# Retention, forgetting and stick-breaking attention in float32: the totals of the last 16 keys in one half-height matmul for each bank, the forgetting tail in column groups

## The chip, the cores and the metric

The kernel runs on one NeuronCore of one Trainium2 chip. The metric is the device time of one execution in microseconds (us). Before the change it is 1461.64 us, the median of 3 runs (1461.39 to 1462.56).

## The reference

The input is 256 tokens of 1024 features. The first block puts 16 learned tokens ahead of them (272 in all), and then comes a mixer of two halves, retention with 4 heads and forgetting attention with 8 heads, and a gated feed-forward network with a short convolution. The second block puts 16 other learned tokens in place of the first and runs two layers, each with a feed-forward network, a mixer (stick-breaking attention with 8 heads of 64, beside a convolution over 31 tokens) and another feed-forward network. All of it is float32. Two parts matter here:

```python
# stick-breaking attention, second block, 8 heads, 2 layers
z = jnp.einsum('bhqd,bhkd->bhqk', qb, kh) * scale
valid = key_pos < qpos
log_keep = jnp.where(valid, jax.nn.log_sigmoid(-z), 0.0)
after = lax.cumsum(log_keep, axis=3, reverse=True) - log_keep
attn = jnp.where(valid, jnp.exp(jax.nn.log_sigmoid(z) + after), 0.0)

# forgetting attention, first block, 8 heads
logits = jnp.einsum('bqhd,bkhd->bhqk', qf[:, q0:q1], kf[:, :q1]) * scale
bias = c[:, :, q0:q1, None] - c[:, :, None, :q1]
logits = jnp.where(mask[None, None], logits + bias, NEG)
p = jax.nn.softmax(logits, axis=-1)
outs.append(jnp.einsum('bhqk,bkhd->bqhd', p, vf[:, :q1]))
```

## The kernel before, in words

**The projections.** Each weight slab (1024 x 128, or 1408 x 128) is split into a rounded high part (`whi`, type fp32r, by ScalarE) and a rounded low part (`wlo`, by VectorE or GpSimd), and so are the activations (`xh`, `xl`). A product is then three single-pass fp32r matmuls for every 128 rows: L1685, L1686 and L1687. These make up most of the program. Each engine has its own instruction stream, written out by hand in Python; semaphores join the streams. There is no scheduler: the order in the streams is the order in the code.

**Where the small matmuls stand.** All other work of TensorE is put between the slabs at fixed slab numbers `s`. 272 tokens are three blocks of 128, 128 and 16. Attention for the last block, of 16 keys or 16 queries, is the tail. Small matmuls go through a helper `mm` (L1837), so the trace shows that line for nearly all of them; the tiles and shapes tell them apart. The scratch tensor `scr` holds, among others, `prob`, `probT`, `qz`, `keep` and `attn`; `ax` holds the split activations and, at that time, `keep_hi` and `keep_lo`. XP and XQ are two PSUM tiles of two banks each, called X[0] to X[3].

**Stick-breaking attention** (`mixer`, four slabs or phases for each pair of heads c, from slab 14 on; in the prediction such a turn is a round). `scores(c)` writes the logits of two heads into X[0] and X[1]: keys on the partitions, 432 columns for the three key blocks. ScalarE and VectorE turn them into `keep` (minus the log of the keep factor). ScalarE rounds it to `keep_hi` (L870) and GpSimd makes `keep_lo`, the rest (L518). `sums(c)` adds the reverse cumulative sum over keys: four matmuls of 432 columns with a triangle of -1 (`later_r`), then the totals of later key blocks with a matrix of -1 (`minus_r`): four of 144 columns and four of 32 columns. The last four bring the total of the last 16 keys to the 16 last queries of the two earlier blocks. Their right-hand side is 128 rows high, though only 16 rows hold keys; the others hold zeros. `values(c)` multiplies with the values. In these phases VectorE also evacuates each slab, and runs the 31 taps of the convolution (L1488) in the time that is left.

**Forgetting attention, the tail.** The 16 last queries of all 8 heads are put side by side on 128 partitions (`qz`, zero outside each head's own 16 columns). `tail_logits` (slab 14) adds a mask, the decay and four matmuls of 272 columns, one for each pair of heads, all into the 128 x 272 output. `tail_values(c)` (slabs 18 to 21) multiplies the 128 value features of a pair of heads with the 32 probability columns of that pair, three matmuls for the three key blocks; the part that mixes one head's features with the other's queries is never read.

A matmul may take fewer than 128 rows of weights (lower height, a row group) or fewer than 128 columns (a column group, whose output goes to the same partitions). The kernel already does so in `scores` (two heads, 64 rows each), in the retention's `ret_products` (four heads, 32 rows each), and in `fox_values` and `values` (two heads, 64 columns each).

Of the kernel before, what the change touches and what calls it, by code (L numbers as in the profile page):

```python
# [27 lines left out]
F32 = mybir.dt.float32  # L28
F32R = mybir.dt.float32r
ALU = mybir.AluOpType  # L30
ACT = mybir.ActivationFunctionType


P = 128
# [3 lines left out]
T = META + SEQ  # L38
# [7 lines left out]
CC = 4  # L46
# [15 lines left out]
SBW, SB_SEG = 432, 144  # L62

FOX_A, FOX_B, FOX_W = slice(0, P), slice(P, 3 * P), 3 * P
# [112 lines left out]
FV, FQ, FK, RQ, RK, RV, RG = 0, 4, 5, 12, 14, 16, 20  # L177
# [5 lines left out]
def build(nc, hT, meta2, w8, w11, fbias, prm_d, cst1_d, cst_d, gain_d, out_d):  # L183
    ctx = ExitStack()
    with ctx:
        def sb(name, shape, dt=F32):
            return ctx.enter_context(nc.sbuf_tensor(name, shape, dt))
# [24 lines left out]
        eps = sb("eps", [P, 3])  # L212
        tok_sum, tok_pre, tok_rec = sb("tok_sum", [P, 5]), sb("tok_pre", [P, 3]), sb("tok_rec", [P, 2])
        acc = sb("acc", [P, T])
        sq = sb("sq", [P, 2, T])
        rinv = sb("rinv", [P, T])
        gmix = sb("gmix", [P, 2 * DC])
# [240 lines left out]
        @block.gpsimd  # L458
        def _(pool):
            def lo(g, j, cols):  # L460
                pool.wait_ge(hi_ready[j], g + 1)
                pool.tensor_tensor(wlo[:, j, 0:cols], raw[:, j, 0:cols], whi[:, j, 0:cols].bitcast(F32),  # L462
                                   ALU.subtract).then_inc(lo_ready[j], 1)

            def los(n, g, kind):
                cols, slots = kind
                with pool.Fori(0, n) as i:
                    for j in slots:
                        lo(g + i, j, cols)

            def first_los(g):

                for j in SHARED:
                    lo(g, j, S8)

            for k, value in enumerate((EPS, EPS * EPS, LN_EPS)):
                pool.memset(eps[:, k:k + 1], value).then_inc(eps_set, 1)
            wff = prm[:, PRM_WFF:PRM_WFF + DC * FOX_H]
            pool.wait_ge(prm_landed, 16)
            pool.tensor_copy(wffr[:, 0, :], wff).then_inc(gate_step, 1)  # L480
            pool.wait_ge(gate_step, 1)
            pool.tensor_tensor(wffr[:, 1, :], wff, wffr[:, 0, :].bitcast(F32), ALU.subtract).then_inc(gate_step, 1)
            lo(0, 2, S8)
            lo(0, 3, S8)
            lo(1, 0, S8)
            lo(1, 1, S8)
            pool.wait_ge(ff_step, 2)
            lo(1, 2, S8)
            pool.wait_ge(cst_landed, 16)
            pool.tensor_copy(identr[:, :], ident).then_inc(hide_ready, 1)  # L490
            pool.tensor_copy(hider[:, :], hide).then_inc(hide_ready, 1)
            pool.tensor_copy(later_r[:, :], minus_later).then_inc(hide_ready, 1)
            pool.tensor_copy(selr[:, :], ident[0:P, 0:FOX_H]).then_inc(gate_step, 1)
            pool.wait_ge(gate_step, 3)
            pool.tensor_copy(selr[FOX_LO, :], ident[FOX_LO, FOX_LO]).then_inc(gate_step, 1)
            pool.wait_ge(gate_step, 4)
            pool.tensor_copy(tailr[:, :].rearrange("p (h q) -> p h q", h=FOX_H),
                             selr[:, :].bitcast(F32).rearrange("p (h q) -> p h q", q=1).to_broadcast(
                                 [P, FOX_H, T - 2 * P])).then_inc(mask_ready, 1)
            pool.memset(qz[:, :, :], 0.0).then_inc(qz_zero, 1)  # L500
            pool.memset(proj[:, FQ:FK + 2 * CC - 1, 0:T_A], 0.0).then_inc(q_zero, 1)
            lo(1, 3, S8)
            pool.wait_ge(c1_landed, 16)
            pool.tensor_copy(fmaskr, fmask).then_inc(mask_ready, 1)
            pool.tensor_copy(minus_r[:, :], minus_ones).then_inc(minus_ready, 1)
            los(N_QKV1 - 2, 2, K8A)
            los(1, G_WO1, K8A)
            los(N_DN, G_DN1, K11)
            first_los(G_LAYER)
            for l in range(LAYERS):  # L510
                g = G_LAYER + PER_LAYER * l
                los(N_UP - 1, g + L_UPA + 1, K8S)
                los(N_DN, g + L_DNA, K11)
                with pool.Fori(0, CC) as c:
                    for j in range(3):
                        lo(g + L_MIX + LOW_FROM + c, j, S8)
                    pool.wait_ge(keep_high, CC * l + c + 1)
                    pool.tensor_tensor(keep_lo, keep, keep_hi.bitcast(F32), ALU.subtract).then_inc(keep_low, 1)  # L518
                    lo(g + L_MIX + LOW_FROM + c, 3, S8)
                los(N_UP - 1, g + L_UPB + 1, K8S)  # L520
                if l < LAYERS - 1:
                    los(N_DN, g + L_DNB, K11)
                    first_los(g + PER_LAYER)
                    continue
                for n in range(LAST_SLABS):
                    if n % 4 in SHARED:
                        lo(g + L_DNB + n // 4, n % 4, S8)
# [3 lines left out]
        def _(act):  # L531
# [312 lines left out]
            def mixer(g, l, p, t):  # L844
# [21 lines left out]
                def round_keep(c):  # L866
                    act.wait_ge(keep_ready, CC * l + c + 1)
                    if c:
                        act.wait_ge(cum_mm, CC * l + c)
                    act.activation(keep_hi, keep, ACT.Copy).then_inc(keep_high, 1)  # L870

                def weights(c):

# [131 lines left out]
        def _(dve):  # L1005
# [463 lines left out]
            def mixer(g, l, p, t):  # L1469
# [21 lines left out]
                def keeps(c):  # L1491

                    dve.wait_ge(soft_step, 3 * (CC * l + c) + 3)
                    dve.scalar_tensor_tensor(keep, XP[:, :, 0:SBW], 0.0, keep, ALU.max, ALU.add).then_inc(keep_ready, 1)

                def out_lo(c):
                    dve.wait_ge(o_hi, CC * l + c + 1)
                    dve.tensor_tensor(al[:, c, t:], X[2][:, t:T], ah[:, c, t:].bitcast(F32), ALU.subtract).then_inc(o_lo, 1)

                ga = g + N_MIX  # L1500
                for s in range(4 * N_MIX):
# [47 lines left out]
                                          ALU.mult).then_inc(u_ready, 1)  # L1549
                    if phase == 1 and 0 <= pair < CC:  # L1550
                        keeps(pair)
                    if s < LN_FROM:
                        taps(s)

# [117 lines left out]
        def _(pe):  # L1672
# [163 lines left out]
            def mm(out, lhsT, rhs, start):  # L1836
                return pe.matmul(out, lhsT, rhs, start=start, stop=True, skip_group_check=True)  # L1837
# [94 lines left out]
            def tail_logits():  # L1932
                pe.wait_ge(fp_ready, 2 * FOX_PAIRS)
                pe.wait_ge(qz_ready, 2 * CC)
                pe.wait_ge(c_ready, 6)
                out = X[0][:, 0:T]
                mm(out, identr[:, :], fmaskr[:, FOX_W:], True)
                mm(out, tailr[:, :], csumr, False)
                for c in range(CC):
                    ins = mm(out, qz[:, c, :], proj[:, FK + 2 * c, :], False)  # L1940
                ins.then_inc(fl_mm, 1)

            def fox_turn(i):
# [27 lines left out]
            def tail_values(c):  # L1971

                pe.wait_ge(rs_ready, 6 if c else 2)
                if c >= 2:
                    pe.wait_ge(ro_sq, c - 1)
                w = 2 * (T - 2 * P)
                for b in range(3):
                    ins = mm(X[3][:, FOX_W + w * c:FOX_W + w * c + w], vT[:, b, P * c:P * c + P],
                             probT[:, 0, P * b + w * c:P * b + w * c + w], b == 0)
                if c == CC - 1:  # L1980
                    ins.then_inc(fo_mm, 1)

# [116 lines left out]
            def mixer(g, l, t):  # L2099
# [18 lines left out]

                def sums(c):

                    pe.wait_ge(keep_low, CC * l + c + 1)
                    tail, mid = T - 2 * P, SB_AT[0] + P
                    for part in (keep_hi, keep_lo):
                        for bank in range(2):
                            mm(X[bank][:, 0:SBW], later_r[:, :], part[:, bank, :], False)
                    if c == 0:
                        pe.wait_ge(minus_ready, 1)
                    for part in (keep_hi, keep_lo):
                        for bank in range(2):
                            mm(X[bank][:, mid:SB_AT[1]], minus_r[:, :], part[:, bank, SB_AT[1]:SBW], False)  # L2130
                    for part in (keep_hi, keep_lo):
                        for bank in range(2):
                            both = X[bank][:, mid:SBW].rearrange("p (s n) -> p s n", n=SB_SEG)[:, :, P:SB_SEG]
                            last = part[:, bank, 0:tail].rearrange("p (s n) -> p s n", s=1).to_broadcast([P, 2, tail])
                            ins = mm(both, minus_r[:, :], last, False)
                    ins.then_inc(cum_mm, 1)

                def values(c):
# [204 lines left out]
```

## Time and profile before

| | |
|---|---|
| median of 3 runs | 1461.64 us |
| profiled execution | 1462.14 us |
| its span | 1460.3 us |
| VectorE busy | 903.3 us (62%) |
| ScalarE busy | 767.8 us (53%) |
| GpSimd busy | 493.8 us (34%) |
| TensorE clock granted | 0.999 of full |
| DMA | 250.92 MB, mean 172 GB/s |

In the profile PE is TensorE (matmuls), PEld its weight loads, DVE VectorE, ACT ScalarE, POOL GpSimd. Busy time is the union of an engine's instructions over the span. The end of a matmul in the profile is modelled, and matmuls overlap, so the time that one costs is read from the start or the end of one to that of the next. Of the profiled execution's 1462.14 us the span covers 1460.3 us.

### The profile page before, as it was taken

To read this page: it belongs to the slowest core of one execution; us is meant where nothing else is said; L and a number is where in the kernel's file an instruction comes from. 1 tells how busy PE (TensorE), PEld (TensorE's weight loads), DVE (VectorE), ACT (ScalarE), POOL (GpSimd) and SP (SyncE) were. 2 spreads that over 40 slices of the span, in tenths; PEclk is the share of its full clock that TensorE was granted. 3 is DMA by queue.
4 is the path that set the end of the run, shared out by engine and by line. 5 is a ranking of instruction groups with operands and counts; after the bars stand their busy time and mean duration, and the time that the engine had idled before them with its cause. 6 is when DMAs were issued, how large, how long until landed. Compare 5 with 4: busy or idle time off the path is not lost.

```text
span 1460.3 us, 30910 instructions
## 1 busy us (share of the span) xinstructions
PE 1452.9 (99%) x11465; PEld 1421.6 (97%) x11465; DVE 903.3 (62%) x1576; ACT 767.8 (53%) x1097; POOL 493.8 (34%) x212
## 2 busy tenths in 40 slices
PE   9999999999999999999999999999999999999998
PEld 8999999889999999999999999999999999999987
DVE  6438888756445469988644434444447898864533
ACT  6556565555444446567544544444444657654443
POOL 6551000533334303710333442433420570044342
PEclk9999999999999999999999999999999999999999
DMA  7435566645556445445555654555644545567663
GB/s 262 137 102 160 176 196 192 213 157 172 173 172 212 163 130 165 141 156 162 175 176 172 207 180 129 183 173 183 199 151 145 173 118 186 174 193 202 208 189 114
DMA packets 74635, 250.92 MB, mean 172 GB/s; under 512 B 15809, under 2 KB 16705, under 8 KB 74561
## 3 DMA queue, kind: packets, MB, share of 16 engines
q1 hardware_dynamic: 74272, 249.38, 54.6%
q8 instruction: 49, 0.80, 0.2%
q10 hardware_dynamic: 288, 0.54, 0.1%
q14 instruction: 26, 0.20, 0.0%
HBM read 247.79 MB, written 1.05 MB: 170 GB/s over the span
## 4 chain that ended last, share of the span: by engine, by line
PE 98%; DVE 1%; ACT 0%; issue 0%; DVEq 0%; ACTq 0%
PE W L1685 27%; PE W L1686 27%; PE W L1687 27%; PE W L1773 3%; PE XP L1837 3%; PE XQ L1837 2%; PE W L1772 1%; PE W L1737 1%; PE W L1788 1%; PE W L1787 1%; PE W L1738 1%; PE W L1786 1%; PE W L1739 1%; PE XQ L1949 0%; PE XP L1842 0%
## 5 line engine op out<-in xcount | busy, mean ns | idle before, releaser
L462 POOL TENSOR_TENSOR wlo<-raw,whi 128x1024 fp32r<-128x1024 f32 (+1 forms) x185 | 473.2, 2562 | 915.4 <-ACT whi L536 914.9
L1685 PE MATMUL W<-xh,whi 128*128 128x272 f32 (+2 forms) x2400 | 689.8, 287 | 0.0
L1686 PE MATMUL W<-xl,whi 128*128 128x272 f32 (+2 forms) x2400 | 687.0, 286 | 0.0
L1687 PE MATMUL W<-xh,wlo 128*128 128x272 f32 (+2 forms) x2400 | 685.9, 286 | 0.0
L536 ACT ACTIVATE whi<-raw 128x1024 fp32r<-128x1024 f32 (+1 forms) x440 | 480.9, 1098 | 128.9 <-PE W L1687 89.6
L1685 PEld LDWEIGHTS W<-xh,whi 128*128 128x128 f32 x2400 | 452.3, 188 | 2.2 <-issue 1.2
L1687 PEld LDWEIGHTS W<-xh,wlo 128*128 128x128 f32 x2400 | 452.1, 188 | 0.0
L1686 PEld LDWEIGHTS W<-xl,whi 128*128 128x128 f32 x2400 | 451.3, 188 | 0.2
L1011 DVE TENSOR_TENSOR wlo<-raw,whi 128x1024 fp32r<-128x1024 f32 (+1 forms) x255 | 331.7, 1302 | 80.5 <-ACT whi L536 80.1
L1685 PE MATMUL W<-ax,whi 128*128 128x272 f32 (+2 forms) x816 | 234.4, 287 | 0.4 <-DVE ax L1455 0.3
L1686 PE MATMUL W<-ax,whi 128*128 128x272 f32 (+2 forms) x816 | 234.4, 287 | 0.0
L1687 PE MATMUL W<-ax,wlo 128*128 128x272 f32 (+2 forms) x816 | 234.3, 287 | 0.0
L1686 PEld LDWEIGHTS W<-ax,whi 128*128 128x128 f32 x816 | 154.8, 190 | 0.0
L1685 PEld LDWEIGHTS W<-ax,whi 128*128 128x128 f32 x816 | 153.6, 188 | 0.9 <-issue 0.5
L1687 PEld LDWEIGHTS W<-ax,wlo 128*128 128x128 f32 x816 | 153.4, 188 | 0.0
L1027 DVE TENSOR_TENSOR scr<-W,rinv 128x272 f32<-128x272 f32 (+2 forms) x140 | 60.3, 431 | 113.7 <-PE W L1687 113.1
L586 ACT ACTIVATE ax<-W 128x272 f32 (+3 forms) x88 | 34.7, 395 | 180.4 <-DVE W L1098 180.4
L583 ACT ACTIVATE scr<-scr 128x272 f32<-128x272 f32 (+1 forms) x110 | 46.9, 426 | 107.8 <-DVE scr L1027 76.5
L1027 DVE TENSOR_TENSOR W<-W,rinv 128x272 f32<-128x272 f32 (+1 forms) x88 | 39.1, 444 | 93.3 <-PE W L1687 93.3
L1488 DVE SCALAR_TENSOR_TENSOR XQ<-scr,prm,XQ 128x272 f32<-128x272 f32 (+1 forms) x184 | 91.3, 496 | 5.3
L560 ACT ACTIVATE sq<-h 128x272 f32 (+3 forms) x48 | 20.4, 426 | 99.9 <-DVE h L1046 99.9
L1046 DVE SCALAR_TENSOR_TENSOR h<-W,h 128x272 f32<-128x272 f32 (+3 forms) x48 | 20.7, 434 | 80.0 <-PE W L1687 78.0
(288 smaller groups left out, 1405.1 us busy)
## 6 DMA issues: line engine op xcount, KB each, us to landing
raw<-in_w SPq DMA_DIRECT2D x377, 512.0 KB, 3.7
raw<-in_w SPq DMA_DIRECT2D x64, 704.0 KB, 4.1
proj<-proj SPq DMA_DIRECT2D x16, 64.0 KB, 3.6
scr<-in_cst SPq DMA_DIRECT2D x1, 1000.0 KB, 8.6
h<-in_hT SPq DMA_DIRECT2D x3, 272.0 KB, 5.2
raw<-in_w SPq DMA_DIRECT2D x2, 256.0 KB, 4.1
proj<-in_gain SPq DMA_DIRECT2D x1, 512.0 KB, 4.6
out<-proj SPq DMA_DIRECT2D x4, 128.0 KB, 1.8
```

Of the source, the lines that this page charges most:

```text
L462: pool.tensor_tensor(wlo[:, j, 0:cols], raw[:, j, 0:cols], whi[:, j, 0:cols].bitcast(F32), ALU.subtract).then_inc(lo_ready[j], 1)
L536: act.activation(whi[:, j, 0:cols], raw[:, j, 0:cols], ACT.Copy).then_inc(hi_ready[j], 1)
L583: act.activation(actv[:, b, t:], gate[:, b, 2 + t:T + 2], ACT.Silu).then_inc(act_ready, 1)
L586: act.activation(ah[:, bass.ds(c, 1), t:], gated(b, conv, t), ACT.Copy).then_inc(ah_ready, 1)
L1011: dve.tensor_tensor(wlo[:, slot, 0:cols], raw[:, slot, 0:cols], whi[:, slot, 0:cols].bitcast(F32), ALU.subtract).then_inc(lo_ready[slot], 1)
L1027: return dve.tensor_tensor(out, W[bank][:, t:T], rinv[:, t:], ALU.mult)
L1488: ins = dve.scalar_tensor_tensor(total, u[:, c, k + t:k + T], w, total, ALU.mult, ALU.add)
L1685: pe.matmul(out, whi[:, j, w], mh, start=start and k == 0, stop=False, skip_group_check=True)
L1686: pe.matmul(out, whi[:, j, w], ml, start=False, stop=False, skip_group_check=True)
L1687: ins = pe.matmul(out, wlo[:, j, w], mh, start=False, stop=stop and k == len(rhs) - 1, skip_group_check=True)
L1773: ins = pe.matmul(both, whi[:, j, w], ax[:, c, :, T_B:], start=False, stop=c == FC - 1, skip_group_check=True)
L1837: return pe.matmul(out, lhsT, rhs, start=start, stop=True, skip_group_check=True)
```

## The change

There are three parts.

1. A new tile `keep_last`, 128 x 16, holds for bank 0 in its rows 0 to 63 and for bank 1 in its rows 64 to 127 the first 32 rows of the last key block's `keep`: 32 rows rounded (ScalarE, two instructions behind `keep_hi`) and 32 rows of the rest (VectorE, two subtractions in `last_lo`, behind the evacuation of phase 2). The four matmuls of `sums` with 128 rows become two with 64 rows, one for each bank. `keep_high` and `keep_low` count three steps for each pair in place of one, and the sums wait for both.
2. `tail_logits`: the matmul of head pair c takes only the 32 columns of `qz` that belong to it and writes only its 32 partitions.
3. `tail_values`: each matmul becomes two, one for each head, of 64 weight columns and 16 columns of probabilities.

```diff
         acc = sb("acc", [P, T])
+        keep_last = sb("keep_last", [P, T - 2 * P], F32R)
...
-                    pool.wait_ge(keep_high, CC * l + c + 1)
+                    pool.wait_ge(keep_high, 3 * (CC * l + c) + 1)
...
                     act.activation(keep_hi, keep, ACT.Copy).then_inc(keep_high, 1)
+                    for bank in range(2):
+                        act.activation(keep_last[64 * bank:64 * bank + 32, :], keep[0:32, bank, 0:T - 2 * P],
+                                       ACT.Copy).then_inc(keep_high, 1)
...
+                def last_lo(c):
+
+                    dve.wait_ge(keep_high, 3 * (CC * l + c) + 1)
+                    if c:
+                        dve.wait_ge(cum_mm, CC * l + c)
+                    for bank in range(2):
+                        dve.tensor_tensor(keep_last[64 * bank + 32:64 * bank + 64, :], keep[0:32, bank, 0:T - 2 * P],
+                                          keep_hi[0:32, bank, 0:T - 2 * P].bitcast(F32), ALU.subtract).then_inc(keep_low, 1)
...
+                    if phase == 2 and 0 <= pair < CC:
+                        last_lo(pair)
                     if s < LN_FROM:
                         taps(s)
...
                 for c in range(CC):
-                    ins = mm(out, qz[:, c, :], proj[:, FK + 2 * c, :], False)
+                    rows = slice(32 * c, 32 * c + 32)
+                    ins = mm(out[rows, :], qz[:, c, rows], proj[:, FK + 2 * c, :], False)
...
                 for b in range(3):
-                    ins = mm(X[3][:, FOX_W + w * c:FOX_W + w * c + w], vT[:, b, P * c:P * c + P],
-                             probT[:, 0, P * b + w * c:P * b + w * c + w], b == 0)
+                    for half in range(2):
+                        p0, q0, q1 = 64 * half, w * c + w // 2 * half, w * c + w // 2 * (half + 1)
+                        ins = mm(X[3][p0:p0 + 64, FOX_W + q0:FOX_W + q1], vT[:, b, P * c + p0:P * c + p0 + 64],
+                                 probT[:, 0, P * b + q0:P * b + q1], b == 0)
...
-                    pe.wait_ge(keep_low, CC * l + c + 1)
+                    pe.wait_ge(keep_high, 3 * (CC * l + c + 1))
+                    pe.wait_ge(keep_low, 3 * (CC * l + c + 1))
...
-                    for part in (keep_hi, keep_lo):
-                        for bank in range(2):
-                            both = X[bank][:, mid:SBW].rearrange("p (s n) -> p s n", n=SB_SEG)[:, :, P:SB_SEG]
-                            last = part[:, bank, 0:tail].rearrange("p (s n) -> p s n", s=1).to_broadcast([P, 2, tail])
-                            ins = mm(both, minus_r[:, :], last, False)
+                    for bank in range(2):
+                        p0 = 64 * bank
+                        both = X[bank][:, mid:SBW].rearrange("p (s n) -> p s n", n=SB_SEG)[:, :, P:SB_SEG]
+                        last = keep_last[p0:p0 + 64, :].rearrange("p (s n) -> p s n", s=1).to_broadcast([64, 2, tail])
+                        ins = mm(both, minus_r[p0:p0 + 64, :], last, False)
```

TensorE's stream at the first sums of the first layer, before and then with the change; `keep_low` and `keep_high` are the semaphores of the rounded parts, and the L1685 row is the next slab.

```order
2194 L1837 MATMUL XP<-ax,later_r 128x432 [waits keep_low]
2195 L1837 MATMUL XP<-ax,later_r 128x432 x3
2196 L1837 MATMUL XP<-ax,minus_r 128x144 [waits minus_ready]
2197 L1837 MATMUL XP<-ax,minus_r 128x144 x3
2198 L1837 MATMUL XP<-ax,minus_r 128x2x16 x4
2199 L1685 MATMUL W<-xh,whi 128x272 [waits lo_ready2,evac_done]
```

In the changed program the same place reads:

```order
2194 L1852 MATMUL XP<-ax,later_r 128x432 [waits keep_low,keep_high]
2195 L1852 MATMUL XP<-ax,later_r 128x432 x3
2196 L1852 MATMUL XP<-ax,minus_r 128x144 [waits minus_ready]
2197 L1852 MATMUL XP<-ax,minus_r 128x144 x3
2198 L1852 MATMUL XP<-keep_last,minus_r 128x2x16 x2
2199 L1700 MATMUL W<-xh,whi 128x272 [waits lo_ready2,evac_done]
```

Two of the four small matmuls are gone, the other two read `keep_last`, and the first one of the sums waits for a second semaphore. The line numbers of the changed program are 15 higher here.

VectorE's stream in the same round before the change: the softplus (`soft_step`), the taps (`conv_step`), the evacuation of phase 2 (`proj<-W,rinv`), taps, and the next evacuation.

```order
416 L1494 SCALAR_TENSOR_TENSOR scr<-XP,scr 128x864 [waits soft_step]
417 L1488 SCALAR_TENSOR_TENSOR XQ<-scr,prm,XQ 128x272 [waits conv_step] x5
418 L1536 SCALAR_TENSOR_TENSOR proj<-W,rinv 128x272 [waits mm_done]
419 L1488 SCALAR_TENSOR_TENSOR XQ<-scr,prm,XQ 128x272 [waits conv_step] x4
420 L1027 TENSOR_TENSOR scr<-W,rinv 128x272 [waits mm_done]
```

With the change VectorE's stream there is:

```order
416 L1498 SCALAR_TENSOR_TENSOR scr<-XP,scr 128x864 [waits soft_step]
417 L1492 SCALAR_TENSOR_TENSOR XQ<-scr,prm,XQ 128x272 [waits conv_step] x5
418 L1549 SCALAR_TENSOR_TENSOR proj<-W,rinv 128x272 [waits mm_done]
419 L1506 TENSOR_TENSOR keep_last<-scr,ax 32x16 [waits keep_high]
420 L1506 TENSOR_TENSOR keep_last<-scr,ax 32x16
421 L1492 SCALAR_TENSOR_TENSOR XQ<-scr,prm,XQ 128x272 [waits conv_step] x4
422 L1031 TENSOR_TENSOR scr<-W,rinv 128x272 [waits mm_done]
```

The two subtractions stand between the evacuation and the taps, and the first waits for the rounded part of ScalarE.

## Rows read from the trace of the kernel before

**Rows 1.** The page, parts 1 and 4: busy us, share, passes; the chain by engine.
```profile
PE 1452.9 (99%) x11465; PEld 1421.6 (97%) x11465; DVE 903.3 (62%) x1576; ACT 767.8 (53%) x1097; POOL 493.8 (34%) x212
PE 98%; DVE 1%; ACT 0%; issue 0%; DVEq 0%; ACTq 0%
```

**Rows 2.** TensorE's timeline, scores of pair 1, narrow windows: start, length, shape, passes.
```profile
585.73 0.29 PE L1837 MATMUL XP<-hider,identr 128*128 128x288 f32 x1
585.95 0.50 PE L1837 MATMUL XP<-proj,scr 64*128 64x272 f32 x2
...
586.28 0.40 PE L1837 MATMUL XP<-proj,scr 64*128 64x272 f32 x2
...
585.95 1.10 PE L1837 MATMUL XP<-proj,scr 64*128 64x272 f32 x12
```

**Rows 3.** TensorE's timeline, values of pair 0 and the slab behind them.
```profile
586.98 0.45 PE L1837 MATMUL XQ<-scr,vT 128*64 128x272 f32 x2
...
587.77 0.21 PE L1837 MATMUL XQ<-scr,vT 128*64 128x16 f32 x1
587.90 0.39 PE L1685 MATMUL W<-xh,whi 128*128 128x272 f32 x1
```

**Rows 4.** TensorE's timeline, first passes of the retention's scores.
```profile
82.74 0.50 PE L1837 MATMUL XP<-proj 32*128 32x272 f32 x2
82.75 0.50 PE L1837 MATMUL XQ<-proj 32*128 32x272 f32 x2
```

**Rows 5.** TensorE's timeline, end of the first sums and the slab behind them.
```profile
581.74 0.50 PE L1837 MATMUL XP<-ax,minus_r 128*128 128x144 f32 x3
...
582.38 0.26 PE L1837 MATMUL XP<-ax,minus_r 128*128 128x32 f32 x1
582.49 0.37 PE L1685 MATMUL W<-xh,whi 128*128 128x272 f32 x1
```

**Rows 6.** TensorE's timeline, before and behind the tail values of pair 2.
```profile
92.03 0.29 PE L1687 MATMUL W<-xh,wlo 128*128 128x272 f32 x1
...
92.75 0.48 PE L1837 MATMUL XQ<-scr 128*128 128x272 f32 x1
```

**Rows 7.** TensorE's timeline, the tail's logits and the first transpose behind them.
```profile
69.63 0.28 PE L1837 MATMUL XP<-ax,tailr 128*128 128x272 f32 x1
69.76 2.00 PE L1837 MATMUL XP<-proj,scr 128*128 128x272 f32 x8
...
71.59 0.27 PE L1949 MATMUL XQ<-cst,scr 128*128 128x128 f32 x1
```

**Rows 8.** Groups by form, TensorE: passes, busy us together, mean ns.
```profile
L1837 PE MATMUL XQ<-scr,vT 128*64 128x16 f32 x32 | 2.0, 194 | 0.0
```

**Rows 9.** Groups by form: small operations of ScalarE and VectorE.
```profile
L727 ACT ACTIVATE scr<-proj 64x16 f32<-64x16 f32 x8 | 1.7, 210 | 0.1
...
L1146 DVE TENSOR_TENSOR scr<-scr 128x32 f32<-128x32 f32 x1 | 0.2, 194 | 0.0
...
L1336 DVE TENSOR_TENSOR scr<-scr 128x2 f32<-128x2 f32 x4 | 2.7, 676 | 0.1
```

**Rows 10.** Timelines of four engines, last layer; idle time, releaser in brackets.
```profile
1199.29 1.06 ACT L536 ACTIVATE whi<-raw 128x1024 fp32r<-128x1024 f32 x1 [0.55 <-PE W L1687]
...
1165.57 0.44 DVE L1027 TENSOR_TENSOR scr<-W,rinv 128x272 f32<-128x272 f32 x1 [0.85 <-PE W L1687]
...
1180.97 0.42 DVE L1027 TENSOR_TENSOR proj<-W,rinv 128x256 f32<-128x256 f32 x1
...
1196.39 0.42 DVE L1027 TENSOR_TENSOR proj<-W,rinv 128x256 f32<-128x256 f32 x1 [0.20 <-PE W L1687]
...
1200.19 0.42 DVE L1027 TENSOR_TENSOR proj<-W,rinv 128x256 f32<-128x256 f32 x1
...
1198.82 2.05 POOL L518 TENSOR_TENSOR ax<-scr,ax 128x864 fp32r<-128x864 f32 x1 [3.96 <-ACT ax L870]
...
1201.87 0.94 PE L1837 MATMUL XP<-ax,later_r 128*128 128x432 f32 x4
```

## The prediction

> **What bounds the kernel now.** I read four views, in this order. First the page's busy times and its chain of waits: TensorE is busy 99% of the span and is 98% of the chain that ended last [rows 1]. So a change counts by what it does to TensorE's own stream, and work on the other engines is free unless TensorE comes to wait for it. Second the groups by form, to size the small matmuls. Third the timeline of TensorE in narrow windows, at each of the three places that the diff touches and at the places where the kernel already uses half-height, quarter-height or half-width matmuls: these tell what such a matmul costs and what it costs to go over to it and back. Fourth the timelines of the other three engines just ahead of the sums, for the slack of the new rounding steps.
>
> A plain float32 matmul is two passes in the trace, one with rounded operands (fp32r) is one. A pass is counted here by its end, since passes overlap: 1452.9 us for 11465 passes are 0.127 us from one end to the next [rows 1], although a 272-column pass is 0.29 us long.
>
> **The price of a change of mode.** In the scores, full-height passes are followed by half-height ones. The last full one ends at 585.73 + 0.29 = 586.02; the first two half-height passes, one in each half, start at 585.95 and take 0.50 us where the next two take 0.40, because their weights are loaded first, with nothing beside them [rows 2]. They end at 586.45, so the first pass of the new mode ends its own length plus 0.03 us after the last of the old one. Going back it is the same: the last half-width pass ends at 587.77 + 0.21 = 587.98, the first full one at 587.90 + 0.39 = 588.29, its own 0.29 plus 0.03 [rows 3]. For a 272-column pass that is 0.32 us in place of 0.127: each switch costs 0.2 us. Into half-width passes it is a little less: the half-height passes end at 585.95 + 1.10 = 587.05 and the first two half-width ones at 586.98 + 0.45 = 587.43, own length (0.40) less 0.02 [rows 2, 3]. What the modes give is shown too: passes in different row groups run side by side. The quarter-height passes of four heads, two into XP and two into XQ, start within 0.02 us of each other and all end by 83.25 [rows 4].
>
> The Trainium skill says the same of the switch in TensorEngine Tiling (Array Packing), Key Properties: a change of tiling mode drains the engine; it gives no price. The same page's table of theoretical speedups (up to 2x for a half, 4x for a quarter) knows no such cost, and by it the change would come out as in my second rival. The rows above side with the drain.
>
> **Sums over the last 16 keys** (8 executions: 4 head pairs in 2 layers). Before, four full-height fp32r passes of 32 columns stand behind the last 144-column pass. They start 0.11 us apart (582.38, and the projection's 582.49), not the 0.015 that 32/272 of 0.127 would be, because each waits for 128 columns of weights. From the end of the last 144-column pass (581.74 + 0.50 = 582.24) to the end of the first projection pass (582.49 + 0.37 = 582.86) it is 0.62 us [rows 5]. After, two half-height passes in different row groups take their place: 0.19 us (the length of a small pass, 194 ns for 16 columns [rows 8]) plus 0.01 for the second, plus 0.03 for going over, and then 0.29 + 0.03 for going back: 0.55 us. That is 0.07 us less, and 0.06 in unrounded reading; 8 x 0.06 = 0.5 us less. The trace has no fp32r pass at half height, so the bounds are: with no overlap the second comes 0.11 us later, +0.05 x 8 = +0.4 us; with no price for the switch three intervals of 0.11 go, -0.33 x 8 = -2.7 us. I take -0.5, by the scores, which are the nearest rows.
>
> **Forgetting logits of the tail** (once). Before, eight full passes of 272 float32 columns take 2.00 us, (2.00 - 0.39) / 7 = 0.23 us apart. From the end of the pass before them (69.63 + 0.28 = 69.91) to the end of the first transpose behind them (71.59 + 0.27 = 71.86) it is 1.95 us [rows 7]. After, each head pair writes its own 32 partitions with 32 columns of weights. If all four column groups run side by side, as the four row groups of [rows 4] do, two rounds are left: 0.39 + 0.02 for four starts, less 0.02 for going over (from half-width passes), plus 0.23, plus 0.27 + 0.03 for going back: 0.92 us, 1.0 us less. Bounds: side by side by twos, as the half-width passes show for two groups, 0.46 more, so -0.6; none side by side, 8 x 0.23 as before and two switches, +0.3; no price for the switch, 6 x 0.23 = -1.4. I take -1.0.
>
> How long 32 columns of weights take at full height no row here shows. The Trainium skill, TensorE: Matmul & The Clock Gate, section LDWEIGHTS, has it as columns over 1.2 GHz whatever the rows, so an estimate of 0.03 us, against 0.05 for 64; by it the sum would be 0.03 us better still.
>
> **Values of the tail** (4 executions). Before, six full passes of 32 columns. From the end of the projection before them (92.03 + 0.29 = 92.32) to the end of the first pass behind them (92.75 + 0.48 = 93.23) it is 0.91 us [rows 6]. After, twelve passes of 16 columns with 64 columns of weights, in two column groups: six pairs. The trace has such pairs in the stick-breaking values: 8 groups of four passes take 2.0 us together, 0.25 each, so with 0.19 for a pass and 0.01 for its partner a further pair adds 0.05 [rows 8]. That makes 0.19 + 0.01 - 0.02 + 5 x 0.05 = 0.43, and 0.39 + 0.03 for going back (0.39 is the length of such a pass once its weights lie ready, as in the logits): 0.85 us, 0.06 less. Where the transposes follow instead, in the first of the four, I count nothing. I take -0.1 for all four, rounded down. Bounds: twelve passes in a row at 0.05, 0.27 more each, +0.8; no price for the switch, where six steps of 0.11 become 0.05, -0.3 each, -1.2.
>
> **What lies beside.** ScalarE gets two rounding copies of 32 x 16 behind the big one, 16 in all. The nearest row has 0.21 us for 64 x 16 [rows 9], so 0.42 a round, and ScalarE then idles 0.55 us before its next weight rounding [rows 10]: covered. VectorE gets two subtractions a round, between the evacuation and the taps (order rows in the section on the change); the nearest row has 0.19 us for 128 x 32 [rows 9], 0.38 a round. Queued behind them are taps and later evacuations. VectorE's idle time, in which it caught up, is 0.85 us before the second round's softplus in the last layer, then none that the view shows, and 0.20 [rows 10]. So it falls behind by 0.38, then 0.56, and with the fourth pair 0.94 us. TensorE wants the pieces at 1201.87, VectorE's evacuation in the same round begins at 1200.19 and takes 0.42: 1.26 us of lead [rows 10]. GpSimd's low part ends at 1198.82 + 2.05 = 1200.87, 1.0 us ahead, and would be 0.56 late. TensorE waits for neither. The added semaphore wait stands in front of the same matmul as the old one, and behind it is only TensorE's own stream. If this cover were gone, each us of lateness at the fourth sums would be one us of the total.
>
> **The sum.** -0.5 - 1.0 - 0.1 = -1.6 us. The profiled execution took 1462.14 us (span 1460.3), so 1460.5; the median of before is 0.5 us below that execution, so on the scale of the medians 1461.64 - 1.6 = 1460.0 us. This is 0.1%, inside the 0.2% (2.9 us) that a measurement of this kernel can tell from no change.
>
> **Rivals.** *The pieces do not overlap.* Only plain float32 passes are seen side by side, in two or four row groups or two column groups; fp32r and four column groups are not. Then each split only adds passes and switches: +0.4 + 0.3 + 0.8 = +1.5 us, 1463.1, slower than before. Against it: every tiled pass in the trace overlaps. It decides once the pieces that run one after the other cost more than the 1.6 us of the forecast, so over half of them.
> *The switch costs nothing here.* For it: the weights are the same minus_r that is already loaded in full, and the switch's price is seen only with plain float32 on its tiled side. Then -2.7 - 1.4 - 1.2 = -5.3 us, 1456.3: faster. Against it: the row of the scores has a price although fp32r stands ahead, and the way back leads into fp32r.
> *VectorE is late.* Among its small operations one kind takes 0.68 us for 128 x 2 [rows 9]. At that price a round costs 1.36 us; in the last layer it is behind by 0.51, 1.87, 3.03, and 4.39 with the fourth pair, less 1.26 of lead: TensorE waits 3.1 us by the fourth sums, and at most as much in the layer before, of which I take two thirds. With the 1.6 gained, 3.1 + 2.1 - 1.6 = +3.6 us, 1465.2: slower. It decides from 6x - 0.20 = 1.26, x = 0.24 us for one operation (two in each of three rounds that are not made up for); the nearest row, at 0.19, is not far below.
>
> **How the numbers follow.** The forecast, side by side and with the price of the switch, 0.74 (with the logits by twos, 1460.4, inside it). No overlap 0.09, no price 0.10, VectorE late 0.05; 0.02 for others. The forecast's own range is 1459.2 to 1460.9, from the bounds of the logits and a rounding of 0.05 us in each of eight sums; with the medians' spread of 0.5 us and half of the no-overlap case it is 1458.7 to 1462.3. Faster by over 0.2% takes the no-price case and little else: 0.11. Slower by over 0.2% takes VectorE, and the no-overlap case only with bad luck: 0.06. Same: 0.83.
>
> **What would show it.** In the profile after: two passes on keep_last 0.01 us apart, the load before them 0.07 us ahead of the end of the last 144-column pass, and 0.54 us to the end of the first projection pass. Eight 32-row logits passes in about 0.65 us. Twelve 64 x 16 passes of the tail values in about 0.5 us. No idle time of TensorE before the first pass on later_r. A logits group of over 1 us would speak for twos or none; a wait on VectorE's keep_last for the third rival; sums that shrink by 0.3 us each for the second.

## The result

| | before | after |
|---|---|---|
| median of the runs | 1461.55 us (4 runs, 1461.39 to 1462.56) | 1478.75 us (4 runs, 1477.85 to 1481.77) |
| profiled execution, span, clock | 1462.14, 1460.3, 0.999 | 1481.77, 1479.6, 0.994 |

The ratio is 1.012, interval 1.0102 to 1.0137: 17.2 us slower. The prediction had 1460.0 us, range 1458.7 to 1462.3, and slower at 0.06. It was wrong, and the time lies outside its range. The profiled execution of the changed kernel is the slowest of its four. Two runs further down, one of e_full_height (1545.33 us, clock 0.85) and one of the kernel before beside it (2190.09 us, clock 0.598), were slow ones, and the ratios leave them out.

The changed kernel's page, busy times and chain by engine:

```profile
PE 1459.9 (99%) x11473; PEld 1425.3 (96%) x11473; DVE 923.8 (62%) x1592; ACT 770.2 (52%) x1113; POOL 494.1 (33%) x212
...
PE 91%; DVE 7%; issue 1%; ACT 0%; DVEq 0%; ACTq 0%
```

Against [rows 1], VectorE has 16 instructions more and 20.5 us more busy time: 1.3 us for an instruction of 32 x 16. It was 1% of the chain and is now 7%. TensorE's waits for other engines in the changed kernel (us in total, times, longest), the two longest rows:

```profile
PE XP L1852 <- DVE keep_last L1506: 12.2, 8, 2.3
PE XP L1852 <- DVE vT L1252: 1.2, 1, 1.2
```

The second row is in the kernel before with the same numbers; the first is new. All eight sums wait for VectorE's rounded low part. The instructions that write it (shortest, median and longest ns, from the first to the last):

```profile
L1506 DVE TENSOR_TENSOR keep_last<-scr,ax x16: 172/1278/2311, 577.6 to 1215.7; 32x16 fp32r<-32x16 f32 x16
...
L873 ACT ACTIVATE keep_last<-scr x16: 196/206/214, 575.5 to 1213.7; 32x16 fp32r<-32x16 f32 x16
```

ScalarE's copies are all alike, at 0.21 us. VectorE's subtractions are of two kinds, one of each in every round: 0.17 to 0.28, and 2.28 to 2.31 us. The median lies between the kinds and describes neither. The timelines of VectorE and, below the last dots, of GpSimd around the first pair's sums (start, length; the second row and the last are from narrower windows):

```profile
577.15 0.43 DVE L1549 SCALAR_TENSOR_TENSOR proj<-W,rinv 128x272 f32<-128x272 f32 x1
577.62 0.17 DVE L1506 TENSOR_TENSOR keep_last<-scr,ax 32x16 fp32r<-32x16 f32 x1
...
577.62 2.51 DVE L1506 TENSOR_TENSOR keep_last<-scr,ax 32x16 fp32r<-32x16 f32 x2
580.05 1.02 DVE L1492 SCALAR_TENSOR_TENSOR XQ<-scr,prm,XQ 128x272 f32<-128x272 f32 x2
...
575.70 2.06 POOL L519 TENSOR_TENSOR ax<-scr,ax 128x864 fp32r<-128x864 f32 x1 [3.35 <-ACT ax L871]
577.72 4.73 POOL L463 TENSOR_TENSOR wlo<-raw,whi 128x1024 fp32r<-128x1024 f32 x2
...
577.72 2.38 POOL L463 TENSOR_TENSOR wlo<-raw,whi 128x1024 fp32r<-128x1024 f32 x1
```

GpSimd's `keep_lo` (L519) ends at 577.76. The first subtraction begins at 577.62 and takes 0.17 us. Then GpSimd runs two weight subtractions (L463), the first from 577.72 to 580.10. VectorE's second subtraction is marked as busy from 577.82 on, just behind that start, and ends at 580.13, 0.03 us after GpSimd's. The taps (L1492) stand behind it. All eight rounds look like this. On TensorE the same stretch is:

```profile
580.27 1.02 PE L1852 MATMUL XP<-ax,later_r 128*128 128x432 f32 x4 [1.00 <-DVE keep_last L1506]
...
581.43 0.28 PE L1852 MATMUL XP<-ax,minus_r 128*128 128x144 f32 x1
581.63 0.28 PE L1852 MATMUL XP<-keep_last,minus_r 64*128 64x32 f32 x2
581.85 0.40 PE L1700 MATMUL W<-xh,whi 128*128 128x272 f32 x1
```

From the end of the last 144-column pass (581.71) to the end of the first slab pass (582.25) it is 0.54 us, against 0.62 in [rows 5] and 0.55 foretold. TensorE's side of the change does what the prediction says, behind a wait that it had ruled out.

The waits have a sequel. Two stretches behind waits of the last layer (of 1.9 and 2.3 us) and a long stretch of that layer in the changed kernel, then the same 65 us of the kernel before (length; busy PE, PEld, DVE, ACT, POOL; granted clock; DMA share; GB/s):

```profile
1182.93:1187.36 4.43, 4.43 (x22) 4.43 (x21) 4.15 (x10) 0.89 (x1) 1.88 (x1) 0.50 0.64 191
1220.95:1224.95 4.00, 4.00 (x21) 4.00 (x19) 2.96 (x6) 1.31 (x2) 0.00 (x0) 0.50 0.34 123
...
1160.00:1225.00 65.00, 58.27 (x437) 55.38 (x437) 59.42 (x112) 30.53 (x39) 36.93 (x17) 0.89 0.37 113
```

```profile
1160.00:1225.00 65.00, 65.00 (x564) 63.29 (x564) 57.70 (x117) 41.62 (x48) 31.07 (x14) 1.00 0.49 147
```

In these two stretches TensorE has no idle time and still runs at 0.50, its lower level (1.2 GHz). That is so behind three of the eight waits, the third one in the first layer; behind the other five the clock stays up. Over the 65 us TensorE makes 437 passes instead of 564.

The pages tell what the loss is made of in the profiled executions. TensorE's busy time and its idle time (span less busy time) are 1452.9 and 7.4 us before, 1459.9 and 19.7 after. So of the 19.3 us by which the span grew, 12.3 are idle time, the eight waits, and 7.0 are passes that take longer.

### The profile page after: what moved, and what is told of

It reads as the page before. It is cut to its first block, busy times and chain, and to the rows that moved or that the text cites. A ratio compares the mean times of both kernels' runs of the same rounds, so it can differ in the third digit from the quotient of the medians.

```text
span 1479.6 us, 30972 instructions
## 1 busy us (share of the span) xinstructions
PE 1459.9 (99%) x11473; PEld 1425.3 (96%) x11473; DVE 923.8 (62%) x1592; ACT 770.2 (52%) x1113; POOL 494.1 (33%) x212
## 4 chain that ended last, share of the span: by engine, by line
PE 91%; DVE 7%; issue 1%; ACT 0%; DVEq 0%; ACTq 0%
PE W L1700 25%; PE W L1701 25%; PE W L1702 25%; DVE XQ L1492 4%; PE W L1788 3%; PE XP L1852 2%; PE XQ L1852 1%; PE W L1787 1%; DVE keep_last L1506 1%; PE W L1752 1%; PE W L1803 1%; PE W L1802 1%; PE W L1753 1%; PE W L1801 1%; PE W L1754 1%
## 5 line engine op out<-in xcount | busy, mean ns | idle before, releaser
L463 POOL TENSOR_TENSOR wlo<-raw,whi 128x1024 fp32r<-128x1024 f32 (+1 forms) x185 | 473.5, 2564 | 931.4 <-ACT whi L537 930.9
L1492 DVE SCALAR_TENSOR_TENSOR XQ<-scr,prm,XQ 128x272 f32<-128x272 f32 (+1 forms) x184 | 91.2, 496 | 5.3
```

The source lines that it names most:

```text
L1492: ins = dve.scalar_tensor_tensor(total, u[:, c, k + t:k + T], w, total, ALU.mult, ALU.add)
```

## The experiments

Two readings were open. One: a VectorE instruction with two inputs in SBUF waits until the GpSimd instruction that is running has ended. The other: the second subtraction is slow in itself, by its rows (96 to 127) or its operation. And of the total: how much is VectorE's lost time, how much TensorE's clock.

### TensorE's two edits without the sums: e_tails

The kernel before, with only the edits of the logits and of the tail values.

> Only the two edits of the forgetting tail (logits in four column groups, values in two); the sums are as before. Theory P (the slowdown comes from VectorE's two subtractions, which wait for GpSimd because both read two SBUF inputs) and theory Q (the subtraction that writes from partition 96 is slow by itself) both leave this part alone: the trace of the changed kernel has the logits group 1.08 us shorter and the values about 0.05 us longer or shorter each, so 1.0 to 1.2 us under before, 1460.4 us. A theory T, that the tail edits cost something that shows later (clock, late softmax), gives over 1461.6.

Measured: 1460.86 us (11 runs, 1460.19 to 1461.5) against 1461.79 (21 runs), ratio 0.9994 (0.9985 to 1.0003). That is 0.9 us less where 1.1 were foretold, with an interval that does not exclude no change. None of the 17 us is here.

### The two subtractions alone: e_subs_only, e_subs_nowait

```
+dve.wait_ge(keep_high, CC * l + c + 1)
+for bank in range(2):
+    dve.tensor_tensor(keep_last[64*bank+32:64*bank+64, :], keep[0:32, bank, 0:T-2*P], keep_hi[0:32, bank, ...], ALU.subtract).then_inc(extra_low, 1)
 ...
+pe.wait_ge(extra_low, 2 * (CC * l + c + 1))     # e_subs_only, at the sums
+act.wait_ge(extra_low, 2 * (CC * l + c))        # e_subs_nowait: no wait on PE
```

> The kernel before with only VectorE's two subtractions added, and TensorE waiting for them at the sums; no matmul is changed (the two results are not used). P and Q: TensorE waits about 12.2 us in eight places as in the changed kernel and loses 4 to 8 us to the clock: 1461.55 + 17 to 20 = 1478.5 to 1481.5 us. Theory H (the half-height matmuls, or the switch to them, bring part of the loss): clearly less, under 1475 us.

Measured: 1481.05 us (4 runs) against 1461.79, ratio 1.0127 (1.0112 to 1.0143). The two subtractions and the wait, with the matmuls of before, cost 19.3 us: they are the whole loss. TensorE's wait:

```profile
PE XP L1848 <- DVE keep_last L1502: 12.8, 8, 2.2
```

> As the run with the two subtractions alone, but TensorE does not wait for them (only ScalarE does, 10 us later, before it overwrites what they read). Theory W, that the time is lost in TensorE's direct wait for the two pieces: 1461.8 to 1463 us, nothing is left of the slowdown. Theory D, that VectorE's lost time itself is what counts (2.3 us a round held back, 0.3 us of own work, against 0.2 to 0.85 us of idle time a round, so that its taps, its evacuations and the softplus of the next round come late): three rounds a layer pass on 7.9 us less some 1.5 of idle time and 1 of lead, about 5 us in each layer, so 1471 to 1473 us; the sums then wait for GpSimd's low part, which waits for the softplus.

Measured: 1475.69 us (4 runs) against 1461.85, ratio 1.0098 (1.0083 to 1.0114). Without TensorE's wait for them, 13.8 us of loss remain, more than the 1471 to 1473 that the theory of VectorE's lost time had foretold: its kind is right, its size too small. TensorE waits at the sums all the same, for what stands behind the subtractions:

```profile
PE XP L1850 <- POOL ax L520: 9.1, 6, 2.2
```

So taking the wait on the two pieces away from TensorE would not have saved the change: VectorE has lost the time, its softplus of the next round comes late, and GpSimd's low part, which stands behind it, comes late too.

### Is it GpSimd that it waits for? e_pool_holds, e_swap

```
 pool.tensor_tensor(keep_lo, keep, keep_hi.bitcast(F32), ALU.subtract).then_inc(keep_low, 1)
+pool.wait_ge(keep_low, 3 * (CC * l + c) + 3)
 lo(g + L_MIX + LOW_FROM + c, 3, S8)
```

GpSimd holds its next weight tile back until both subtractions are done. All else is the changed kernel.

> The changed kernel with one wait added: GpSimd starts its next weight subtraction only when VectorE's two pieces are done. VectorE's instructions, their place and their operands are the same. P: both subtractions take about 0.2 us, TensorE waits for none of them, its clock stays up: 1461.55 - 1.1 (tails) - 0.5 (sums) = 1460.0 us. Q: the second subtraction still takes 2.3 us and the time stays at 1478 to 1480 us.

Measured: 1460.93 us (11 runs, 1460.32 to 1464.44), ratio 0.9998 (0.9989 to 1.0007). The 16 subtractions:

```profile
L1507 DVE TENSOR_TENSOR keep_last<-scr,ax x16: 168/169/280, 577.7 to 1199.6; 32x16 fp32r<-32x16 f32 x16
```

One added wait on an engine that is busy a third of the time takes 17.8 us off the changed kernel. The first subtraction takes 0.17 to 0.28 us and the second 0.17 in every round, and TensorE's waits list no `keep_last`.

The swapped order (`for bank in (1, 0)`), one execution:

> The changed kernel with the order of VectorE's two subtractions turned round: first the one that writes from partition 96, then the one that writes from partition 32. P: again the first is short (0.17 to 0.28 us), since GpSimd's instruction is just ending, and the second one long (2.3 us), since GpSimd's next one has begun. Q: now the first one, which writes from partition 96, is the long one.

Measured: 1477.65 us. The first subtraction, now that of bank 1 on rows 96 to 127, takes 0.17 to 0.28 us, and the second, now on rows 32 to 63, 2.27 to 2.31. The group, and the two of the first round:

```profile
L1506 DVE TENSOR_TENSOR keep_last<-scr,ax x16: 169/1276/2307, 578.1 to 1214.6; 32x16 fp32r<-32x16 f32 x16
...
578.08 0.17 DVE L1506 TENSOR_TENSOR keep_last<-scr,ax 32x16 fp32r<-32x16 f32 x1
...
578.27 2.29 DVE L1506 TENSOR_TENSOR keep_last<-scr,ax 32x16 fp32r<-32x16 f32 x1
```

Not the rows, but the place in time decides. With e_pool_holds, where the same operation takes 0.17 us, the second reading falls.

### Which operands wait: e_psum_input, e_one_input

In e_psum_input the second input is a 32 x 16 piece of PSUM, so the low rows hold other numbers. In e_one_input it is one input in SBUF, times 1.0, and the low rows hold the whole value. (ScalarE's part and the matmuls stay.)

```
-dve.tensor_tensor(keep_last[...], keep[0:32, bank, ...], keep_hi[0:32, bank, ...].bitcast(F32), ALU.subtract)
+dve.tensor_tensor(keep_last[...], keep[0:32, bank, ...], W[0][0:32, t:t + T - 2 * P], ALU.subtract)   # e_psum_input
+dve.tensor_scalar(keep_last[...], keep[0:32, bank, ...], 1.0, None, ALU.mult)                          # e_one_input
```

> The changed kernel, but VectorE's two subtractions take their second input from PSUM (the slab bank W[0] that VectorE has just evacuated) in place of keep_hi in SBUF; the low rows then hold other numbers, only the time counts. Place, shape, output and what else runs are the same. P in its sharp form (only an instruction with two inputs in SBUF waits for GpSimd; the taps, with one in SBUF and one in PSUM, run beside GpSimd at their usual length): both take about 0.2 us, 1460 to 1461 us. If any VectorE read of SBUF of this kind waits, the second one still takes 2.3 us: 1478 us.

> The changed kernel, but each subtraction is a product with 1.0 of the single input keep (the low rows then hold keep itself). One SBUF input, no PSUM. If two SBUF inputs are what makes it wait: about 0.2 us each and 1460 to 1461 us. If a single-input instruction on float32 in SBUF waits for GpSimd as well: 2.3 us for the second one, 1478 us.

Measured: e_psum_input 1460.69 us (10 runs, 1460.19 to 1461.07), ratio 0.9991 (0.9981 to 1.0); e_one_input 1479.27 us (one execution). The first row is of e_psum_input, the second of e_one_input:

```profile
L1506 DVE TENSOR_TENSOR keep_last<-scr,W x16: 159/162/165, 578.1 to 1199.7; 32x16 fp32r<-32x16 f32 x16
```

```profile
L1506 DVE TENSOR_SCALAR keep_last<-scr x16: 169/1280/2304, 578.1 to 1216.2; 32x16 fp32r<-32x16 f32 x16
```

With the same operation, count, place and semaphores, an input from PSUM takes the wait away from all 16. GpSimd is as busy as in the changed kernel, and the second subtraction lies inside its instruction. In e_psum_input, VectorE and then GpSimd:

```profile
578.26 0.17 DVE L1506 TENSOR_TENSOR keep_last<-scr,W 32x16 fp32r<-32x16 f32 x1
...
578.16 7.11 POOL L463 TENSOR_TENSOR wlo<-raw,whi 128x1024 fp32r<-128x1024 f32 x3
```

The output lies in SBUF here too, so with two inputs it is the read that waits, not the write. With one float32 input in SBUF and no second the wait is there in full. The Trainium skill, VectorE: DVE Perf Modes, section Two Vector instructions with no wait between them, says that VectorE's second SBUF read interface is shared with GpSimd, and names as its users instructions with two SBUF inputs or in a two-port mode. The first run agrees for two inputs, 2.3 us against 0.16. The second would then be a float32 instruction in such a mode; its trace shows the wait, not the mode.

### TensorE's clock: e_filler

```
+s = SB_FROM + 4 * c + 3
+pe.wait_ge(evac_done, 4 * g + s - 2)
+for _ in range(12):
+    mm(W[(s + 1) % 4][:, 0:240], identr[:, :], hider[:, 0:240], True)
 pe.wait_ge(keep_high, 3 * (CC * l + c + 1))
```

> The changed kernel with twelve matmuls of 240 columns, whose result is overwritten, ahead of the wait of each sums: about 1.25 us of work inside a wait of 1.0 to 2.3 us. If the half clock in the stretches behind the waits comes from TensorE's idle time, it stays at full clock: 1461.55 - 1.6 + 12.4 (waits, a little filled over) = 1472.4 us. If it has another cause, such as the load on the other engines, the time stays at 1478 to 1479 us.

Measured: 1476.63 us (4 runs, 1476.09 to 1477.14), ratio 1.0103 (1.0088 to 1.0119), where 1472.4 was foretold. The wait and the 65 us of the last layer:

```profile
PE XP L1852 <- DVE keep_last L1506: 3.9, 6, 1.0
```

```profile
1160.00:1225.00 65.00, 62.49 (x531) 59.77 (x530) 61.31 (x116) 33.73 (x42) 36.20 (x16) 1.00 0.40 118
```

The clock is whole again, so the idle time had brought it down, but only 2.1 us of 17.2 come back. The fillers and the sums behind them in the first round:

```profile
578.76 1.50 PE L1852 MATMUL W<-hider,identr 128*128 128x240 f32 x12
580.10 0.96 PE L1852 MATMUL XP<-ax,later_r 128*128 128x432 f32 x4
```

The fillers take 1.3 us a round, 10.7 in all, and with the 3.9 us of waits TensorE spends 14.6 us in front of the sums, where the changed kernel waits 12.2: with TensorE quicker, VectorE is waited for longer. Its column stands at 61.31 of 65 us, where the kernel before has 57.70 (the row shown with the result). The expectation had put the slow clock down as a loss of its own; part of it lay beside VectorE's. How large it is differs between executions: the two profiled ones are 5.7 us apart (1481.77 and 1476.09), the medians 2.1.

### The change without its fault: e_act_low, e_one_sub, e_full_height

In e_act_low ScalarE copies the low rows from GpSimd's finished `keep_lo`, and VectorE does nothing:

```
+def low_rows(c):
+    act.wait_ge(keep_low, 3 * (CC * l + c) + 1)
+    for bank in range(2):
+        act.activation(keep_last[64*bank+32:64*bank+64, :], keep_lo[0:32, bank, 0:T-2*P].bitcast(F32), ACT.Copy).then_inc(keep_low, 1)
 ...
-if phase == 2 and 0 <= pair < CC:
-    last_lo(pair)
```

In e_one_sub that is done for bank 1 alone, and VectorE keeps the first subtraction. e_full_height is e_act_low with `keep_last` of 128 rows (32 high, 32 low, 64 of zeros written once), so that the two passes are full-height and nothing changes mode.

> The changed kernel with VectorE's two subtractions gone: ScalarE copies the low rows from GpSimd's keep_lo into keep_last, two copies of 32 x 16 at about 0.2 us, in a stretch where it idled 1.96 us. No VectorE work is added. Theory P/D: VectorE and TensorE run as before, time 1461.8 - 1.1 - 0.5 = 1460.2 us. If something else of the change cost time (semaphores, the rounding copies, the matmuls), it stays over 1462.

> The changed kernel with only the first of the two subtractions on VectorE; ScalarE copies the other bank's low rows from keep_lo. In every round the first one took 0.17 to 0.28 us, since it comes while GpSimd's low part is just ending. If that is the rule of the wait (it lasts until the running GpSimd instruction ends, no longer), the single subtraction is short in all eight rounds and the time is 1460 to 1461 us. If each VectorE instruction of this kind costs about half of the loss, it is near 1469 us.

> As the run before it, but the two matmuls of the last 16 keys keep 128 rows: keep_last has one 128-row column block for each bank, rows 0 to 31 the rounded part, 32 to 63 the rest, 64 to 127 zeros set once. Two passes of four go (0.11 us each) and there is no switch of mode. By the price of a switch read from the trace (own length + 0.03 us, both ways) this beats half height by 0.22 - 0.06 = 0.16 us a round: 1.3 us less over 8 rounds, 1461.8 - 1.1 - 1.8 = 1458.9 us. If the half height is as cheap as full height, the two runs are equal.

| kernel | median us | runs | ratio to before (interval) |
|---|---|---|---|
| e_act_low | 1460.09 | 11 | 0.9987 (0.9977 to 0.9996) |
| e_one_sub | 1460.29 | 10 | 0.9988 (0.9979 to 0.9998) |
| e_full_height | 1459.15 | 11 | 0.9981 (0.9972 to 0.9991) |

The kernel before, beside them, has 1461.85 us (e_act_low, e_full_height) and 1461.79 (e_one_sub). e_act_low is the prediction's case with the cover in place: 1.8 us under before, where the prediction had 1.6. e_one_sub shows that the first subtraction costs nothing that can be told; its eight take:

```profile
L1513 DVE TENSOR_TENSOR keep_last<-scr,ax x8: 165/213/276, 577.9 to 1199.1; 32x16 fp32r<-32x16 f32 x8
```

The end of the sums in e_act_low and in e_full_height:

```profile
579.30 0.95 PE L1858 MATMUL XP<-ax,later_r 128*128 128x432 f32 x4
...
580.58 0.28 PE L1858 MATMUL XP<-keep_last,minus_r 64*128 64x32 f32 x2
580.79 0.40 PE L1706 MATMUL W<-xh,whi 128*128 128x272 f32 x1
```

```profile
579.68 0.95 PE L1861 MATMUL XP<-ax,later_r 128*128 128x432 f32 x4
...
580.87 0.33 PE L1861 MATMUL XP<-keep_last,minus_r 128*128 128x32 f32 x2
581.05 0.37 PE L1709 MATMUL W<-xh,whi 128*128 128x272 f32 x1
```

From the first pass of the sums to the start of the slab it is 1.49 us with half-height passes and 1.37 with full-height ones (579.30 to 580.79, 579.68 to 581.05): 0.12 less, times 8 is 1.0 us, and the medians differ by 0.94 (e_act_low 1459.59 to 1460.35 us, e_full_height 1458.84 to 1459.8 without its run of 1545.33). Half of the rows multiply zeros, and it is faster still. The number of passes is the same; the half-height ones run side by side, but there are two changes of mode, and by the prediction's price for these 0.16 us a round were foretold. e_full_height is the fastest of all: 2.7 us under before, and 0.19%, so near the edge of what can be told.

## Why the prediction was wrong

**TensorE's terms held.** The sums: 0.54 us against 0.55 foretold. The second of the four tail values, the place of [rows 6], has 0.89 against 0.85 foretold and 0.91 before, so a third of its gain of 0.06 came (the row of the projection before them, the twelve passes, the first pass behind):

```profile
90.34 0.29 PE L1702 MATMUL W<-xh,wlo 128*128 128x272 f32 x1
90.56 0.53 PE L1852 MATMUL XQ<-scr,vT 128*64 128x16 f32 x12
91.02 0.50 PE L1852 MATMUL XQ<-scr 128*128 128x272 f32 x1
```

The logits, from 69.05 + 0.28 = 69.33 to 69.85 + 0.33 = 70.18, are 0.85 us against 0.92 foretold and 1.95 before, so all four column groups ran side by side:

```profile
69.05 0.28 PE L1852 MATMUL XP<-ax,tailr 128*128 128x272 f32 x1
69.26 0.67 PE L1852 MATMUL XP<-proj,scr 128*32 128x272 f32 x8
69.85 0.33 PE L1965 MATMUL XQ<-cst,scr 128*128 128x128 f32 x1
```

Both rivals on TensorE's side, that the pieces do not overlap and that the switch costs nothing, fall with these rows, and e_act_low has the sum of the terms: 1.8 us measured, 1.6 foretold.

**The step that failed** is in "What lies beside": "VectorE gets two subtractions a round [...] the nearest row has 0.19 us for 128 x 32 [rows 9], 0.38 a round", and from it "TensorE waits for neither". The round took 2.51 us. Against 0.38 that is 2.1 us lost, 17.0 over eight rounds; the net loss of the change is 17.2 + 1.6 = 18.8. That the two are near each other is a comparison, not an identity: VectorE's lead and its idle time give some back, and TensorE's slow stretches add to it. With 2.51 in place of 1.36 the third rival's own sum gives lateness of 1.66, 4.17, 6.48 and 8.99 us in the last layer, less 1.26 of lead 7.7, and two thirds of that, 5.2, in the layer before: an estimate of 12.9 us, where TensorE waited 12.2. What the passes of the slow stretches add to that had no term in the prediction. The prediction also looked for a wait at the fourth sums alone; one round of 2.51 us is more than the lead, and the first sums already waited 1.00 us.

The price was not wrong for the operation. It was taken from one row without asking what GpSimd did meanwhile. That was to be read in the trace of before, and in a row that the prediction used: its third rival took the 676 ns of 128 x 2 (L1336) as the price of a kind of operation. That mean of four mixes three of 0.16 us and one of 2.21. Of VectorE and, in the last row, of GpSimd, in the kernel before:

```profile
44.75 0.16 DVE L1336 TENSOR_TENSOR scr<-scr 128x2 f32<-128x2 f32 x1
...
36.50 2.21 DVE L1336 TENSOR_TENSOR scr<-scr 128x2 f32<-128x2 f32 x1
...
33.97 4.73 POOL L462 TENSOR_TENSOR wlo<-raw,whi 128x1024 fp32r<-128x1024 f32 x2
```

VectorE's 2.21 us end at 38.71, and GpSimd's pair at 38.70. A tiny operation 14 times as long as its like, which ends with another engine's: that is a wait, and it shows as busy time. With [rows 10] and GpSimd's next row in the kernel before the rest followed, in the last layer:

```profile
1200.84 2.40 POOL L462 TENSOR_TENSOR wlo<-raw,whi 128x1024 fp32r<-128x1024 f32 x1
```

GpSimd's L518 ends at 1200.87 and VectorE's evacuation at 1200.61, so the first subtraction lands at the end of one GpSimd instruction and the second at the start of the next, of 2.4 us. That would have given 2.3 us for the second subtraction of a round.

**The rival "VectorE is late"** (1465.2, chance 0.05) named the right engine and the right consequence, and its threshold, 0.24 us for an operation, was passed by far: the mean was 1.26. Its price was a mean over two kinds, and it let VectorE catch up to the extent of [rows 10]. What the range lacked was a bound from GpSimd's side: a subtraction with two SBUF inputs should have had, as its upper end, the length of GpSimd's longest instruction beside it, 2.4 us.

## What to carry to other kernels

Before you give VectorE a small operation on SBUF data, look at what GpSimd runs at that moment: where GpSimd has begun first, the price here was the rest of GpSimd's instruction, not that of the elements. Print the shortest and the longest of a group beside its mean; a mean far above that of its like may be a few waits that count as busy. The cure was cheap: give the operation to ScalarE (e_act_low), or let GpSimd hold its next long instruction back (e_pool_holds). Where one of the inputs can lie in PSUM, that takes the wait away too; e_psum_input shows the time of it, with other numbers in the low rows.

## What was not expected of the hardware

- A float32 VectorE instruction with a single SBUF input (TENSOR_SCALAR) waits for GpSimd as one with two does (2.3 us for 32 x 16, in the eight rounds of one execution), while one with its second input in PSUM (0.16 us) does not. Nor do the taps, which read PSUM: they take 0.5 us beside GpSimd's next instruction.
- With GpSimd idle a subtraction of 32 x 16 takes 0.17 us; when it begins just ahead of the end of a GpSimd instruction it ends with it (0.17 to 0.28 us), and by the time the next one comes GpSimd's next instruction has begun (577.72 against 577.82), so that it waits for all of it, in all eight rounds.
- For 32-column pieces, a full-height pass half filled with zeros is 0.06 us cheaper than a half-height one that needs the switch (0.12 us for the two).
